# Feed-forward in two parts: hidden activations through DRAM, W_down as seven block products

## The chip, the cores and the metric

One Trainium2 chip, one NeuronCore of it. The number that counts is the device time of one execution of the whole kernel, in microseconds (us). The kernel is a single launch in fp32 data, with every large product done as three bf16 products (high x high, high x low, low x high).

## The reference, cut to what matters

One decoder layer on 2,048 prompt tokens and 64 sample tokens, model width 1,024, hidden width 2,816. The mixer in front (mLSTM heads and dilated attention) is untouched. The change is in the last lines:

```python
hf = rms_norm(x, g_ffn_pre)
f = (jax.nn.silu(hf @ w_gate) * (hf @ w_up)) @ w_down     # 1024 -> 2816 -> 1024
x = x + rms_norm(f, g_ffn_post)
```

## The kernel before

The stages run one after the other; the last, `stage_ffn`, takes about the second half of the span. All of it works on x, transposed in SBUF (`g.x32`, features on partitions in 8 tiles, tokens along the free axis).

**Units.** The hidden width is cut in 22 tiles of 128 columns (m). The prompt's tokens are cut in two pairs of 512-token chunks (q = 0, 1); a unit is one m for one q, so there are 44 units. In a unit the gate and up products of two token chunks, which would be eight block products, are done as seven (`PRODUCTS`, a Strassen-like scheme over [W_gate, W_up] and the token quarters). Each product is 12 matmuls (4 k-tiles x 3 bf16 products) of 128x512. Their order on TensorE is A11, S1, S2, A12, S3, S4, A22. Four of the weight blocks are sums, made by VectorE (`sum_weights`); all seven are split in a high half by ScalarE (`w_split`) and a low half by VectorE. The weight blocks have one buffer each (A22 two), so the next unit's splits are interleaved with this unit's products. Between the products, results leave PSUM: ScalarE copies (`kept`), VectorE adds (`combine_near`, `combine_mid`, `combine_away`), ScalarE does Silu, VectorE multiplies (`hide_away`, `hide_near`). TensorE may start A22 only after `combine_mid`, since both use the same PSUM bank:

```python
pe.wait_ge(combined, 3 * u + 2)
multiply(u, A22, one, False).then_inc(p_done, 1)
```

Units of q = 0 also do the 64 sample tokens: 48 matmuls of 64 columns behind A11.

**Order of the units.** All 22 m with q = 0, then all 22 with q = 1. The seven split weight blocks are therefore made 44 times, and W_gate and W_up are read twice.

**Down.** After each second unit ("part") the two hidden tiles, split in high and low, are multiplied with two row tiles of W_down: 8 token tiles x 2 halves x 2 hidden tiles x 3 = 96 matmuls of 128x512 (`down_tile`), into two PSUM areas of two banks each. VectorE adds each tile's 128x1024 result into SBUF (`add_down`, line 3184). For q = 0 the sample follows (48 narrow matmuls).

**Turnover.** Between q = 0 and q = 1 the token quarters of q = 1 and their sums are made and split (`t_sum_up`, `t_split`, each 128x2048), partly during the last units of q = 0 and between the adds of its last down part (`turn_over`).

**End.** `square` (ScalarE), `inverse_rms` (GpSimd), `finish` (VectorE), `add_to_residual` (a DMA of GpSimd that accumulates in DRAM).

**Queues.** SP loads W_gate and W_up (`load_up`, `load_gate`), each as soon as the splits of the tile before have freed the raw buffer. GpSimd's queue loads W_down. Every engine's instructions are written out in a fixed order and it waits on semaphores in that order.

Of the kernel before, what the change touches and what calls it, by code (L numbers as in the profile page):

```python
# [79 lines left out]
class Sems:  # L80
# [10 lines left out]
    def give_back(self):  # L91

        self._nc.clear_and_free_semaphores(self._taken)
        self._nc.all_engine_barrier()
        self._taken = []
# [2210 lines left out]
PART = 2  # L2306
PARTS = HIDDEN_TILES // PART
UNITS = N_PAIRS * HIDDEN_TILES
# [353 lines left out]
def stage_ffn(nc, g, sems):  # L2662
# [3 lines left out]
    n_rows = [3, 2]  # L2666
    n_down = [PAIR_TILES + 1, PAIR_TILES]
    pair_of = lambda u: u // HIDDEN_TILES
    w_at = lambda u, j: u * PRODUCTS + W_ORDER.index(j) + 1
    made = lambda u, j: u * PRODUCTS + j + 1  # L2670
    first_row = lambda u: u * n_rows[0] if u < HIDDEN_TILES else HIDDEN_TILES * n_rows[0] + (u - HIDDEN_TILES) * n_rows[1]
    silu_at = lambda u, rows: first_row(u) + 1 + ((SAMPLE, NEAR, AWAY), (NEAR, AWAY))[pair_of(u)].index(rows)
    row_at = lambda u, rows: first_row(u) + 1 + ((SAMPLE, AWAY, NEAR), (AWAY, NEAR))[pair_of(u)].index(rows)
    down_at = lambda q, part: (PARTS * n_down[0] + 1 if q else 0) + part * n_down[q]
    SAMPLE_TURNED = PARTS * n_down[0]
    N_FINAL = TILES + 1
    with ExitStack() as ctx:
        sb = lambda n, s, d=F32: ctx.enter_context(nc.sbuf_tensor(n, s, d))
        two = lambda n, s, d=F32: [sb(f"{n}{i}", s, d) for i in range(2)]
        raw_gate, raw_up, raw_down = g.m_w_raw0, g.m_w_raw1, sb("f_raw_down", [P, D_MODEL])  # L2680
        w_sum_area = sb("f_w_sums", [P, 4 * HK * P])
        w_sum = {j: w_sum_area[:, i * HK * P:(i + 1) * HK * P].rearrange("p (k c) -> p k c", k=HK) for i, j in enumerate((S1, S2, S3, S4))}
        w_hi = [[sb(f"f_w_hi{j}", [P, HK, P], BF16)] * 2 if j != A22 else two(f"f_w_hi{j}_", [P, HK, P], BF16)
                for j in range(PRODUCTS)]
        w_lo = [[sb(f"f_w_lo{j}", [P, HK, P], BF16)] * 2 if j != A22 else two(f"f_w_lo{j}_", [P, HK, P], BF16)
                for j in range(PRODUCTS)]
# [4 lines left out]
        t_hi, t_lo = [{**homes, **{j: sb(f"f_t_{n}{j}", [P, HK, CHUNK], BF16)[:, :, :] for j in (B22, T4)},  # L2691
                       X_S2: s_cells[:, i, :, :], X_SD: s_cells[:, 2 + i, :, :]}
                      for i, (n, homes) in enumerate((("hi", g.t_hi), ("lo", g.t_lo)))]
        y_area = sb("f_sums_then_y", [P, 2 * D_MODEL])
        t_sum = y_area[:, :].rearrange("p (k c) -> p k c", k=HK)
        whole = lambda tile: tile[:, :, :].rearrange("p k c -> p (k c)")
        y_homes = [y_area[:, i * D_MODEL:(i + 1) * D_MODEL] for i in range(2)]
        last_homes = [y_homes[1], y_homes[0], whole(raw_up), whole(raw_gate), w_sum_area[:, 0:D_MODEL], w_sum_area[:, D_MODEL:],
                      raw_down[:, :], g.u_area[:, 0:D_MODEL]]
        y_home = lambda f: y_homes[f % 2] if f <= PAIR_TILES else last_homes[f - PAIR_TILES - 1]  # L2700
        near, mid, away = two("f_near", [P, CHUNK]), two("f_mid", [P, CHUNK]), two("f_away", [P, CHUNK])
        squares = mid[0][:, :].bitcast(BF16)
        s_gate = g.k_new[:, 0:NSAMP]
        h_hi, h_lo = [(sb(f"f_h_{n}", [P, PART * PAIR], BF16)[:, :], g.k_new[:, (1 + i) * NSAMP:(2 + i) * NSAMP].bitcast(BF16))
                      for i, n in enumerate(("hi", "lo"))]
        down_hi, down_lo = [area[:, HK * NTOK:HK * NTOK + PART * D_MODEL].rearrange("p (i c) -> p i c", i=PART)
                            for area in (g.mix_m_hi, g.mix_m_lo)]
        y_s = sb("f_y_s", [NSAMP, D_MODEL])
# [739 lines left out]
```

## Time and profile before

| what | value |
|---|---|
| three timed runs | 2625.64, 2623.40, 2623.57 us (median 2623.57) |
| span of the profiled execution | 2616.7 us |
| the profiled execution's own time | not listed apart; the median lies 6.9 us above the span |
| granted TensorE clock, mean | 0.985 |
| busy: TensorE / VectorE / ScalarE / GpSimd | 96% / 67% / 44% / 9% |
| matmul instructions | 16,971 |
| `stage_ffn`: first to last matmul | about 1288 to 2601 us |

Read it so: the span runs from the first to the last instruction. A matmul of 128x512 is shown with 379 ns, but the next one starts 216 ns later, since matmuls are pipelined; the distance from start to start is what one costs in a row. The same holds on a smaller scale for VectorE (0.69 us shown, 0.60 from start to start). "Idle before, releaser" tells what an instruction waited for.

### The profile page before, as it was taken

The numbers are of one execution on the slowest core, as the hardware profiler recorded it, in microseconds if no ns is written. First come the engines' busy times: TensorE is split into PE (matmuls) and PEld (weight loads), VectorE is DVE, ScalarE is ACT, GpSimd is POOL, SyncE is SP. The second block draws the span as 40 slices with busy tenths as digits, with TensorE's granted clock in tenths as the row PEclk, the third lists the DMA queues.
The fourth block names the chain that finished last, engine by engine and source line by source line (L and its number), as shares of the span: only waits on it lengthen the run. The fifth ranks groups of instructions, "written<-read, shape, count | busy, mean of one in ns | idle before, by whom it ended". The sixth has DMA issues, their size and how long they took to land.

```text
span 2616.7 us, 46148 instructions
## 1 busy us (share of the span) xinstructions
PE 2501.4 (96%) x16971; PEld 1433.1 (55%) x17188; DVE 1745.3 (67%) x3772; ACT 1151.2 (44%) x2671; POOL 246.6 (9%) x630
## 2 busy tenths in 40 slices
PE   7999987899999999899899999999999999999997
PEld 4557765476858677555444444444444444444443
DVE  6658886676766767778666665565577666666665
ACT  5558985454545445433433333322243333333233
POOL 1002220011202112211100000000000000000002
PEclk9999998999999999999999999999999999999999
DMA  6431355601111111444221112111111222222213
GB/s 223 135 97 54 104 141 161 189 18 51 34 42 44 35 35 60 145 142 153 73 73 49 51 55 61 53 49 49 49 49 49 57 74 72 66 71 57 57 53 73
DMA packets 203224, 202.92 MB, mean 78 GB/s; under 512 B 11053, under 2 KB 181048, under 8 KB 201584
## 3 DMA queue, kind: packets, MB, share of 16 engines
q1 hardware_dynamic: 193082, 165.26, 21.1%
q0 software_dynamic: 9920, 34.70, 5.1%
q8 instruction: 139, 2.28, 0.4%
q14 instruction: 83, 0.68, 0.1%
HBM read 156.86 MB, written 43.06 MB: 76 GB/s over the span
## 4 chain that ended last, share of the span: by engine, by line
PE 43%; DVE 4%; ACT 2%; issue 1%; POOL 0%; POOLq 0%; DVEq 0%; ACTq 0%
PE f_bank L2798 9%; PE f_bank L2797 9%; PE f_bank L2799 9%; PE f_ps_y L120 5%; PE f_ps_y L118 5%; PE f_ps_y L119 5%; ACT f_h_hi L2934 1%; DVE act L3184 1%; DVE f_w_lo L3056 1%; DVE f_h_lo L3110 1%; DVE f_away L3132 1%; DVE f_near L3144 1%; ACT f_w_hi L2916 1%; DVE f_away L3137 0%; DVE f_w_sums L3071 0%
## 5 line engine op out<-in xcount | busy, mean ns | idle before, releaser
L3184 DVE TENSOR_TENSOR act<-act,f_ps_y 128x1024 f32<-128x1024 f32 x170 | 201.9, 1189 | 156.2 <-PE f_ps_y L120 156.1
L2798 PE MATMUL f_bank<-mix_m_lo_then_tokens,f_w_hi 128*128 128x512 bf16 x699 | 264.9, 379 | 1.7
L120 PE MATMUL f_ps_y<-mix_m_hi_then_tokens,f_h_lo 128*128 128x512 bf16 x697 | 264.2, 379 | 0.9
L2799 PE MATMUL f_bank<-mix_m_hi_then_tokens,f_w_lo 128*128 128x512 bf16 x697 | 264.2, 379 | 0.3
L118 PE MATMUL f_ps_y<-mix_m_hi_then_tokens,f_h_hi 128*128 128x512 bf16 x686 | 260.2, 379 | 2.7 <-DVE act L3184 0.3
L119 PE MATMUL f_ps_y<-mix_m_lo_then_tokens,f_h_hi 128*128 128x512 bf16 x687 | 260.4, 379 | 0.9
L2797 PE MATMUL f_bank<-mix_m_hi_then_tokens,f_w_hi 128*128 128x512 bf16 x672 | 254.7, 379 | 0.4
L2951 ACT ACTIVATE f_near<-f_bank 128x512 f32<-128x512 f32 x44 | 26.1, 593 | 430.9 <-PE f_ps_y L120 237.8
L3056 DVE TENSOR_TENSOR f_w_lo<-f_w_sums,f_w_hi 128x512 bf16<-128x512 f32 x176 | 120.9, 689 | 124.3 <-ACT f_w_hi L2916 123.7
L118 PE MATMUL m_ps_then_y<-w_in_then_w_out_lo,act 128*128 128x256 bf16 x640 | 174.4, 273 | 0.1
L119 PE MATMUL m_ps_then_y<-w_in_then_w_out_lo,act 128*128 128x256 bf16 x640 | 174.4, 273 | 0.0
L120 PE MATMUL m_ps_then_y<-w_in_then_w_out_lo,act 128*128 128x256 bf16 x640 | 174.4, 273 | 0.0
L2069 DVE SCALAR_TENSOR_TENSOR y_then_w_out<-z_then_patterns,m_hd,y_then_w_out 128x512 f32<-128x512 f32 x120 | 90.2, 752 | 86.1 <-ACT y_then_w_out L1803 83.3
L119 PE MATMUL m_ps_then_y<-act,w_in_then_w_out_lo 128*128 128x512 bf16 (+1 forms) x400 | 131.9, 348 | 6.5 <-DVE w_in_then_w_out_lo L2036 4.9
L2797 PE MATMUL f_bank<-f_t_hi,f_w_hi 128*128 128x512 bf16 x351 | 133.1, 379 | 4.8 <-DVE f_mid L3126 3.4
L2798 PE MATMUL f_bank<-f_t_lo,f_w_hi 128*128 128x512 bf16 x347 | 131.5, 379 | 0.1
L3020 POOL DMA_DIRECT2D f_raw_down<-in_w_down x44 | 24.6, 560 | 1133.5 <-DVE mix_m_lo_then_tokens L3105 1133.1
L3056 DVE TENSOR_TENSOR f_w_lo<-m_w_raw,f_w_hi 128x512 bf16<-128x512 f32 x132 | 87.2, 688 | 64.5 <-ACT f_w_hi L2916 64.5
L120 PE MATMUL m_ps_then_y<-act,w_in_then_w_out_lo 128*128 128x512 bf16 (+1 forms) x394 | 129.1, 348 | 0.0
L118 PE MATMUL m_ps_then_y<-act,w_in_then_w_out_lo 128*128 128x512 bf16 (+1 forms) x382 | 124.9, 346 | 1.0 <-ACT z_then_patterns L1800 0.7
L2799 PE MATMUL f_bank<-f_t_hi,f_w_lo 128*128 128x512 bf16 x325 | 123.2, 379 | 0.3
L118 PEld LDWEIGHTS f_ps_y<-mix_m_hi_then_tokens,f_h_hi 128*128 128x128 bf16 x704 | 68.8, 98 | 93.7 <-DVE act L3184 12.0
(523 smaller groups left out, 6156.6 us busy)
## 6 DMA issues: line engine op xcount, KB each, us to landing
m_w_raw<-in_w_gate SPq DMA_DIRECT2D x44, 512.0 KB, 4.2
m_w_raw<-in_w_up SPq DMA_DIRECT2D x44, 512.0 KB, 3.9
f_raw_down<-in_w_down POOLq DMA_DIRECT2D x44, 512.0 KB, 3.8
m_w_raw<-in_w_in SPq DMA_DIRECT2D x20, 512.0 KB, 6.1
o_x<-in_x_prompt SPq DMA_DIRECT2D x16, 512.0 KB, 4.4
out_y_prompt<-states_then_x SPq DMA_DIRECT2D x16, 512.0 KB, 3.0
pattern_rows<-a_stage SPq DMA_DIRECT2D x48, 132.0 KB, 2.1
u_then_w_out_then_tokens<-u_rows SPq DMA_DIRECT2D x5, 1024.0 KB, 4.4
```

The costliest lines, as they stand in the source:

```text
L118: pe.matmul(out, w_hi, x_hi, start=first, stop=False, skip_group_check=in_parts)
L119: pe.matmul(out, w_hi, x_lo, start=False, stop=False, skip_group_check=in_parts)
L120: return pe.matmul(out, w_lo, x_hi, start=False, stop=last, skip_group_check=in_parts)
L2069: ins = nc.vector.scalar_tensor_tensor(out, src, w, out, ALU.mult, ALU.add)
L2797: nc.tensor.matmul(bank[:, :], high, t_hi[j][:, k, :], start=first and k == 0, stop=False, skip_group_check=True)
L2798: nc.tensor.matmul(bank[:, :], high, t_lo[j][:, k, :], start=False, stop=False, skip_group_check=True)
L2799: mm = nc.tensor.matmul(bank[:, :], low, t_hi[j][:, k, :], start=False, stop=k == HK - 1, skip_group_check=True)
L2916: nc.scalar.activation(w_hi[j][u % 2][:, :, :], w_from[j], ACT.Copy).then_inc(w_high, 1)
L2934: nc.scalar.activation(h_all(h_hi, u % PART, rows), hidden, ACT.Copy).then_inc(h_high, 1)
L3056: nc.vector.tensor_tensor(w_lo[j][u % 2][:, :, :], w_from[j], w_hi[j][u % 2][:, :, :], ALU.subtract).then_inc(w_low, 1)
L3110: nc.vector.tensor_tensor(low, hidden, high, ALU.subtract).then_inc(h_done, 1)
L3184: nc.vector.tensor_tensor(tile, tile, fresh, ALU.add).then_inc(total_done, 1)
```

## The change

All of it is in `stage_ffn`, with one barrier in front of it.

1. **Order of the units.** m = 0..7 with q = 0 alone; then for m = 8..21 pairs of tiles (m,0), (m,1), (m+1,0), (m+1,1); then m = 0..7 with q = 1 alone. Units that share m in the middle share one weight set (`SET_OF`), so there are 30 sets, not 44. "Solo" units have a set to themselves.
2. **The token quarters of q = 1** are summed and split in units 1 to 6 (`T_STEPS`), into homes of their own.
3. **Hidden activations** are no longer multiplied with W_down at once. Per unit, VectorE sums and ScalarE and VectorE split blocks of them (`hidden_blocks`, `hidden_high`): for even m two blocks (one sum), for odd m five blocks (three sums). SP stores them in DRAM (`store_hidden`).
4. **W_down's four block sums** are made by GpSimd during units 8 to 28 (`sum_down`) and stored in DRAM.
5. **Down as seven products.** After all units: for each of 7 blocks, 8 pairs of token tiles, 11 x 3 matmuls of 128x512 accumulated in one PSUM bank; 6 banks in turn. VectorE adds each 128x512 result into the output tiles (`add_pair`). SP loads the hidden blocks in quarters (`load_hidden`, two DMAs of 720,896 bytes each) into three slots, and 128x512 pieces of W_down or its sums (`load_down`) into four raw buffers; ScalarE and VectorE split the pieces for the next product meanwhile. The first product's 11 pieces are split in the last four units (`TAIL`).
6. The units have two copies of banks 2 and 3, since the down product no longer needs PSUM at the same time.
7. **A barrier** (`give_back`) in front of `stage_ffn` clears and frees the semaphores of the stages before.

The core of the diff:

```diff
-    def give_back(self):
-
-        self._nc.clear_and_free_semaphores(self._taken)
+    def give_back(self, *kept):
+
+        self._nc.clear_and_free_semaphores([s for s in self._taken if not any(s is k for k in kept)])
         self._nc.all_engine_barrier()
...
+SOLO = 8
+UNIT = ([(m, 0) for m in range(SOLO)] + [(m + d, q) for m in range(SOLO, HIDDEN_TILES, 2) for d in range(2) for q in range(N_PAIRS)]
+        + [(m, 1) for m in range(SOLO)])
...
+T_STEPS = {1: [(0, B11), (1, T1)], 2: [(0, T1), (1, T3)], 3: [(0, T3), (0, B21)], 4: [(1, T2), (0, T2)], 5: [(1, T4), (0, T4)], 6: [(0, B22)]}
...
+                def load_hidden(x):
...
+                    sp.wait_ge(h_store[b], 16 * stores_of(b, UNITS if q else LAST_Q0 + 1))
+                    for part, to in enumerate((slot_hi[s], slot_lo[s])):
+                        sp.dma_start(to, g.h_dram[b, q, :, half * 2 + part, :]).then_inc(h_in[s], 16)
...
+                for n in range(UNITS):
+                    if n:
+                        store_hidden(n - 1)
+                    k = SET_OF[n]
+                    if n == USERS[k][-1] and n and k + 2 < N_SETS:
+                        load_up(k + 2)
+                        load_gate(k + 2)
...
+                    if n == UNITS - TAIL:
+                        load_hidden(0)
+                        load_hidden(1)
+                    if n >= UNITS - TAIL:
+                        for i in range((n - UNITS + TAIL) * TAIL_PIECES, min((n - UNITS + TAIL + 1) * TAIL_PIECES, D_PAIRS)):
+                            load_down(i)
...
+                def down_pair(jn, p):
+                    e, x = at_y(jn, p), jn * 4 + p // 2
+                    bank, s = y_bank[e % BANKS], x % H_SLOTS
+                    bank_free(e)
+                    if p % 2 == 0:
+                        pe.wait_ge(h_in[s], 32 * (x // H_SLOTS + 1))
+                    for i in range(D_PAIRS):
+                        if p == 0:
+                            pe.wait_ge(d_low, jn * D_PAIRS + i + 1)
+                        toks = slice(i * 2 * P + p % 2 * P, i * 2 * P + (p % 2 + 1) * P)
+                        mm = product(nc.tensor, bank[:, :], slot_hi[s][:, toks], slot_lo[s][:, toks], d_hi[jn % 2][:, i, :],
+                                     d_lo[jn % 2][:, i, :], i == 0, i == D_PAIRS - 1)
+                    mm.then_inc(y_ready, 1)
...
+                def unit(n):            # ScalarE
...
+                    if n:
+                        hidden_high(n - 1, 0)
+                    act.wait_ge(p_done, made(n, A11))
...
+                    nc.scalar.activation(near[n % SLOTS], bank1[v][:, :], ACT.Copy).then_inc(kept, 1)
...
+                    act.wait_ge(combined, 3 * n + 3)
+                    nc.scalar.activation(away[n % SLOTS], away[n % SLOTS], ACT.Silu).then_inc(silu_done, 1)
+                    if fresh:
+                        w_split(k + 1, S4)
+                    if n >= UNITS - TAIL:
+                        for i in range((n - UNITS + TAIL) * TAIL_PIECES, min((n - UNITS + TAIL + 1) * TAIL_PIECES, D_PAIRS)):
+                            down_high(i)
...
+                def sum_down(i):        # GpSimd; four sums, each stored at once
...
+                    nc.gpsimd.tensor_tensor(down_sum[:, :], b12, b11, ALU.subtract).then_inc(down_step, 1)
+                    pool.wait_ge(down_step, 4 * i + 1)
+                    pool.dma_start(g.down_sums[DOWN_SUMS.index("T1"), i, :, :], down_sum[:, :]).then_inc(down_store, 16)
...
+                def unit(n):            # VectorE
+                    q, k = UNIT[n][1], SET_OF[n]
+                    fresh = n == USERS[k][-1] and k + 1 < N_SETS
+                    hidden_blocks(n - 1)
+                    if n == USERS[k][0] and k + 1 < N_SETS:
+                        w_sum_up(k + 1)
+                    if fresh:
+                        w_split(k + 1, A11)
+                        w_split(k + 1, A22)
+                        w_split(k + 1, S1)
+                        w_split(k + 1, S2)
+                    if q == 0:
+                        sample_hidden(n)
+                    for step in T_STEPS.get(n, ()):
+                        if step[0]:
+                            t_sum_up(step[1])
+                        else:
+                            t_split(1, step[1])
+                    combine_near(n)
+                    if q == 0:
+                        sample_low(n)
+                    if fresh:
+                        w_split(k + 1, A12)
+                    combine_mid(n)
+                    if fresh:
+                        w_split(k + 1, S3)
+                    combine_away(n)
+                    if fresh:
+                        w_split(k + 1, S4)
+                    hide_away(n)
+                    hide_near(n)
+                    if n >= UNITS - TAIL:
...
+                            down_low(i)
...
+            sems.give_back(g.f_gate_in, g.f_up_in, g.t_high, g.t_low, g.t_sums)
```

## Rows read from the trace of the kernel before

**Rows 1.** Windows, q = 1: busy PE, PEld, DVE, ACT, POOL; clock; DMA share; GB/s.
```profile
2043.00:2560.00 517.00, 513.60 (x2339) 232.48 (x2385) 326.71 (x425) 169.29 (x286) 23.82 (x42) 1.00 0.24 64
```
**Rows 2.** Waits in the feed-forward, TensorE and weight loads: us in total, times, longest.
```profile
PE f_bank L2797 <- DVE f_mid L3126: 3.4, 2, 2.6
...
PEld f_ps_y L118 <- DVE act L3184: 12.0, 20, 0.8
```
**Rows 3.** Timeline, TensorE: first matmul of A11 and of S1, unit 24.
```profile
2086.13 0.38 PE L2797 MATMUL f_bank<-u_then_w_out_then_tokens,f_w_hi 128*128 128x512 bf16 x1
...
2088.72 0.38 PE L2797 MATMUL f_bank<-mix_m_hi_then_tokens,f_w_hi 128*128 128x512 bf16 x1
```
**Rows 4.** Chain that ended last (start, us): down parts' first adds, turnover, last add.
```profile
1641.39 1.14 DVE act L3184
...
1702.85 1.14 DVE act L3184
...
1932.89 1.81 ACT u_then_w_out_then_tokens L2923
1934.72 2.15 DVE u_then_w_out_then_tokens L3079
...
2126.65 1.14 DVE act L3184
...
2183.91 1.14 DVE act L3184
...
2601.56 1.23 DVE act L3184
```
**Rows 5.** Timeline, VectorE, unit 24.
```profile
2088.67 0.69 DVE L3071 TENSOR_TENSOR f_w_sums<-m_w_raw 128x512 f32<-128x512 f32 x1
2089.39 0.69 DVE L3071 TENSOR_TENSOR f_w_sums<-f_w_sums,m_w_raw 128x512 f32<-128x512 f32 x1
...
2097.34 0.68 DVE L3120 TENSOR_TENSOR f_near<-f_bank,f_near 128x512 f32<-128x512 f32 x1
2099.24 0.69 DVE L3056 TENSOR_TENSOR f_w_lo<-m_w_raw,f_w_hi 128x512 bf16<-128x512 f32 x1 [1.22 <-ACT f_w_hi L2916]
2099.84 0.68 DVE L3126 TENSOR_TENSOR f_mid<-f_bank,f_mid 128x512 f32<-128x512 f32 x1
...
2101.94 0.69 DVE L3132 TENSOR_TENSOR f_away<-f_bank,f_away 128x512 f32<-128x512 f32 x1 [0.81 <-PE f_bank L2799]
2103.85 0.69 DVE L3056 TENSOR_TENSOR f_w_lo<-f_w_sums,f_w_hi 128x512 bf16<-128x512 f32 x1 [1.22 <-ACT f_w_hi L2916]
2104.46 0.68 DVE L3137 TENSOR_TENSOR f_away<-f_mid,f_away 128x512 f32<-128x512 f32 x1
```
**Rows 6.** Timeline, ScalarE, the same unit.
```profile
2088.92 0.60 ACT L2951 ACTIVATE f_near<-f_bank 128x512 f32<-128x512 f32 x1 [19.21 <-PE f_bank L2799]
...
2098.05 0.63 ACT L2979 ACTIVATE f_near<-f_near 128x512 f32<-128x512 f32 x1 [1.89 <-DVE f_near L3120]
2098.59 0.61 ACT L2916 ACTIVATE f_w_hi<-m_w_raw 128x512 bf16<-128x512 f32 x1
```
**Rows 7.** Page, DMA issues: KB each, median us to landing.
```profile
m_w_raw<-in_w_gate SPq DMA_DIRECT2D x44, 512.0 KB, 4.2
...
a_v<-v_by_key SPq DMA_DIRECT2D x2, 1040.0 KB, 5.8
```
**Rows 8.** Windows: the heaviest DMA traffic, and a gap of TensorE with what followed.
```profile
10.00:20.00 10.00, 6.37 (x30) 4.06 (x30) 8.54 (x14) 7.47 (x15) 0.14 (x1) 1.00 1.02 417
392.00:400.00 8.00, 3.94 (x40) 3.60 (x41) 3.21 (x14) 3.79 (x11) 1.12 (x7) 0.79 0.39 93
```
**Rows 9.** Timeline, TensorE: the first matmul behind that gap.
```profile
396.06 0.19 PE L118 MATMUL a_ps_o<-rows_then_v_then_values,a_pt_hi 128*128 128x65 bf16 x1 [4.23 <-ACT a_stage L719]
```
**Rows 10.** Source view of the one barrier of this kind: the clearing of semaphores.
```profile
L93 POOLq EVENT_SEMAPHORE_RANGE_CLEAR  x1: 634/634/634, 498.2 to 498.2; - x1
```
**Rows 11.** Groups by line, GpSimd: its work on tiles 512 wide.
```profile
L439 POOL COPY a_xn_then_q_cls<-a_x_then_q_st 128x512 bf16<-128x512 bf16 x16 | 18.0, 1123 | 6.1 <-DVE gain_then_q_pairs L866 6.1
```

More of the change, by code:

```diff
@@ L2696, in stage_ffn @@
[L2696 to L2701, printed above, removed]
@@ new lines, in stage_ffn @@
+        near = [hid_area[:, i * PAIR:i * PAIR + CHUNK] for i in range(SLOTS)]
+        away = [hid_area[:, i * PAIR + CHUNK:(i + 1) * PAIR] for i in range(SLOTS)]
+        mid = two("f_mid", [P, CHUNK])
+        squares = mid[0][:, :].bitcast(BF16)
+        h_diff = sb("f_h_diff_then_y_s", [P, CHUNK])
+        y_turned = h_diff[:, :].rearrange("p (k n) -> p k n", k=KT)
+        fifth = [area[:, HK * NTOK:] for area in (g.mix_m_hi, g.mix_m_lo)]
+        h_block = [sb(f"f_h_block{b}", [P, 4, P * 2], BF16)[:, :, :] for b in range(3)]
@@ L2789, in _, with multiply @@
             def _(pe):
[L2790 to L2793 removed]
+                def multiply(n, j, bank, first):
+                    q, k = UNIT[n][1], SET_OF[n]
+                    pe.wait_ge(w_low, w_at(k, j))
+                    if n in (0, FIRST_Q1):
                         pe.wait_ge(t_low, t_at(q, j))
[L2795 to L2800 removed]
@@ L2802, in multiply_sample @@
[L2802 to L2810 removed]
+                    for kt in range(HK):
+                        high, low = w_hi[j][k % 2][:, kt, :], w_lo[j][k % 2][:, kt, :]
+                        nc.tensor.matmul(bank[:, :], high, t_hi[q][j][:, kt, :], start=first and kt == 0, stop=False, skip_group_check=True)
+                        nc.tensor.matmul(bank[:, :], high, t_lo[q][j][:, kt, :], start=False, stop=False, skip_group_check=True)
+                        mm = nc.tensor.matmul(bank[:, :], low, t_hi[q][j][:, kt, :], start=False, stop=kt == HK - 1, skip_group_check=True)
@@ new lines, in multiply, with multiply_sample, sample @@
+                    return mm
+                def multiply_sample(k, j, x, bank, first, last):
+                    for kt in range(HK):
+                        mm = product(nc.tensor, bank, w_hi[j][k % 2][:, kt, :], w_lo[j][k % 2][:, kt, :], t_hi[0][x][:, kt, :],
+                                     t_lo[0][x][:, kt, :], first and kt == 0, last and kt == HK - 1)
+                    return mm
+                def sample(n):
+                    k = SET_OF[n]
+                    pe.wait_ge(w_low, w_at(k, A12))
+                    if n == 0:
```

909 lines of the change are left out of this document (504 added, 405 removed).

## Prediction

> **What bounds the kernel now.** I read the waits first, then windows, then one unit instruction by instruction. In the feed-forward TensorE hardly waits: one window of 517 us has it busy for 513.6 while VectorE is busy for 327 and DMA at a share of 0.24 and 64 GB/s [rows 1]. So the feed-forward lasts as long as its matmuls. A product of 12 matmuls takes 2.59 us from start to start [rows 3], 0.216 us each. A down part follows the next after 61.46 us for q = 0 and 57.26 us for q = 1 [rows 4]; 264 matmuls at 0.216 are 57.02, which leaves 0.24 us lost per part, where the weight loads wait for the adds [rows 2]. The 4.2 us more of q = 0 are 144 narrow sample matmuls, 0.029 each.
>
> **What goes.** The seven units' products stay (44 x 84 matmuls). Down before: 22 parts x 96 = 2112; after: 7 x 8 x 33 = 1848. 264 fewer x 0.216 = **-57.0 us**. The sample keeps its count (1584 narrow ones). The lost 0.24 us at 22 part ends go, since the down product rotates six banks and an add of 0.7 us stands against 33 matmuls of 7.1 us: **-5.3**. The waits of TensorE for `combine_mid` at the turnover go: **-3.4** [rows 2]. The last add is 512 wide, not 1024 (0.69 for 1.23, [rows 4, 5]): **-0.5**. Weight splits of 14 sets go from VectorE and ScalarE; by themselves they are worth nothing, as they lay beside matmuls.
>
> **What the units now cost.** VectorE gets the hidden blocks at the head of each unit. The point that decides is `combine_mid`, which must be over when S4 is: 6 products = 15.55 us behind the unit's start t0, and 16.95 with a sample (48 x 0.029 = 1.4). I lay out VectorE's list by rows: 0.60 per 128x512 instruction, 0.72 where it needs the one before [rows 5], ScalarE 0.52 to 0.54 [rows 6], and from `combine_near`'s start to `combine_mid`'s end 3.18 (Silu, high and low half of A12 lie between: 2097.34 to 2100.52, [rows 5]). `hide_near` of the unit before starts 0.8 behind t0 (`combine_away` 2101.94, its successors to 2104.46, then one slot).
>
> Solo unit, odd tile before it (eight instructions of blocks): `hide_near` 0.8 to 1.5; sums S1, S2, two low halves and S4 to 4.65; low halves of S1, S2 to 5.9; the high half of S4 stands in ScalarE's list behind the copy of product S1 (5.4), so its low half starts at 6.55; four weight sums to 9.7; four splits to 12.1; `combine_mid` over at 15.28. Limit 15.55: it holds, by 0.27. After an even tile (three instructions) it holds by over 1 us. The middle units, with a shared set, have sums and splits in different units and over 2 us spare. Units 1 to 6 also have one or two `t_sum_up` / `t_split` in front of `combine_near`, 2.2 us each (2.15, [rows 4]), their high halves 1.8 to 1.9 on ScalarE behind the split of S2 (10.4). With a sample ScalarE's copies come up to 1.4 later and VectorE waits for them, so it comes to these steps at 11.2 (odd n, three instructions of blocks) or 13.6 (even n, eight):
>
> - n = 1: high half of B11 at 12.3, split 14.5, sum 16.7, `combine_mid` 19.9: 3.0 over the limit 16.95
> - n = 2: 13.6 + 4.4 = 18.0, 21.2: 4.3
> - n = 3: high half at 12.3, two splits 16.7: 3.0
> - n = 4: sum 15.8, high half after it 17.8, split 20.1, 23.2: 6.3
> - n = 5: sum 13.5, high half 15.5, split 17.7, 20.9: 4.0
> - n = 6: 15.8, 19.0: 2.0
>
> Together **+22.6**, less than +15 only if the lists overlap better than in rows, +27 if each handoff is late. The same sum for the last unit of q = 0 before, which has two such instructions, gives 2.5 us; the trace has 2.6 as the longest wait [rows 2]. That is my check of the method.
>
> **The last four units.** At unit 40 SP issues in order: W_gate for set 28 (which waits for the low half of A12, 14.7 behind t0), four hidden loads of 0.72 MB, three pieces of W_down of 0.26 MB. ScalarE's list ends the unit with `down_high(0)`, which waits for the first piece, and behind it stand the hidden blocks and the copy `near` of unit 41, without which S2 cannot start (5.2 behind its t0). 4.2 MB lie before or in that burst. From 1040 KB in 5.8 us and 417 GB/s at best [rows 7, 8] I take 320 GB/s: 13 us, plus 1.5 for the last landing. ScalarE is free about 12 us into unit 41, the copy ends at 13.1, S2 starts 7.9 late. Bounds 5 (417 GB/s) and 12 (250). In unit 42 the 1.8 us of low halves, a little late themselves, meet the margin of 0.27: 2. Together **+10**.
>
> **Clock.** A gap of 4.2 us was followed by a granted clock of 0.79 of 8 us, though idle time and full speed are in that mean [rows 8, 9]. Five gaps of 4 us or more arise (units 2, 4, 5, 41, the barrier); I take 1 us for each, since part of the slow time gives VectorE room: **+4.5**, between 0 and 10.
>
> **Barrier.** 0.63 us for the clearing [rows 10] and drains around it: **+1.5**, between 1 and 4.
>
> **At nothing.** The 512-wide pieces and adds of the down product: 11 splits and 8 adds, some 14 us of VectorE per 57 us product. Stores of hidden blocks: SP is free between two loads. Down's transfers: per product 4 x 1.44 + 11 x 0.26 = 8.6 MB in 57 us, 151 GB/s; the loads run two quarters (14 us each) ahead. If a piece lands late, VectorE's adds queue behind it, covered by six banks. If that cover were gone, each us of lateness would count.
>
> GpSimd's 44 sums are nowhere in the trace; a copy 512 wide took it 1.12 us [rows 11]. They fall in units with spare time on VectorE. Bounds 0 and, were each to hold VectorE for 1.12 us, four per two units against 1.7 us spare: 2.8 x 11 = 31. I take 0, as `combine_near` and `combine_mid` read only one SBUF operand and the sums come in units without splits. The Trainium skill, "SBUF — State Buffer", "Who interferes with whom", speaks against this edit: a VectorE instruction with two SBUF inputs and a GpSimd one that reads SBUF block each other for the whole instruction, and `tensor_tensor` in GpSimd ("GPSIMD Engine Reference") is about half as fast as VectorE's, an estimate of 1.2 us here. By that rule rival B's 10 us would come true; no row of this trace shows such a meeting.
>
> **Sum.** -57.0 - 5.3 - 3.4 - 0.5 + 22.6 + 10 + 4.5 + 1.5 = -27.6. Against the profiled span of 2616.7 that is 2589.1; the median of the timed runs stands 6.9 above the span, so **2596 us**.
>
> **Rivals.**
> A, the stalls do not come: VectorE's order leaves more room, the burst lands in time. -57.0 - 5.3 - 3.4 - 0.5 + 1.5 = -64.7: 2559 us. For it: TensorE never waited long before. Against: the check at the turnover. Chance 0.06.
> B, GpSimd's sums hold VectorE in the middle units: about 10 us (a third of the bound), 2606; with its bound 2627. For it: VectorE has some 16 instructions of 0.60 in each unit of 18.1 us there, more than half its time. Against: the spare time. Chance 0.14.
> C, slower: the down product is bound by its transfers. It takes 415 us of matmuls, sample included, and reads 60 MB. At 130 GB/s it would take 463 us, 48 more: 2644. The gain is gone below 136 GB/s (60 MB in 443 us). For it: two loads and the pieces share one queue, and weight loads of 512 KB land in 4.2 us, 125 GB/s one by one [rows 7]. Against: the 417 GB/s, and several are in flight. Chance 0.08.
> D, the change does not do what it says: the units wait for each other through the DRAM stores (an `h_block` has one buffer), 2 us in each of 44 units: +88, 2684. Against: a store has over 10 us. Chance 0.02.
> My forecast, 2586 to 2608: 0.70.
>
> **Range.** 2584 to 2614: it takes in the bounds of the stalls (-8, +5), the burst (-3, +6), the clock (-4.5, +5.5), and B's likely size. What a measurement of this kernel can tell from no change is about 0.2%, 5 us. Faster by more: forecast, A and most of B, 0.85; within: 0.05; slower: 0.10.
>
> **What would show it.** Matmuls of 128x512 fewer by 264. Waits of TensorE for `f_mid` of 20 to 27 us, in units 1 to 6 alone, unit 4 the longest. One wait of 5 to 12 us in the fourth unit from the end, for ScalarE's copy, ScalarE itself waiting for a DMA into the W_down pieces. Pairs of the down product 7.13 us apart. It would be wrong if even solo units wait at `f_mid` (the margin of 0.27), if the down pairs are further apart, or if GpSimd's sums lengthen VectorE's instructions in units 8 to 28.

## The result, and the profile after

The changed kernel takes **2597.05 us** (median; 2591.45 to 2600.82) beside 2624.61 for the kernel before on the same chip: a ratio of 0.9901, with a 95% interval from 0.9875 to 0.9927, 27.6 us less by the medians. The forecast was 2596 us, also 27.6 less.

The two profiled spans differ by 19.1 us only (2597.6 for 2616.7). The rest lies ahead of the change: over the profiles of this study the last transpose before the feed-forward starts anywhere between 1283.1 and 1291.3 us, here 3.85 us later in the changed kernel than in the one before. So from here on a kernel's **stage** is what I compare: from the start of that transpose to the start of the last add of a product into `g.x32`. Timeline of TensorE, before:
```profile
1284.26 1.11 PE L2428 MATMUL o_turned<-ident,y_then_w_out 64*128 64x64 f32 x8 [7.10 <-DVE y_then_w_out L2650]
1288.13 0.63 PE L2798 MATMUL f_bank<-u_then_w_out_then_tokens,f_w_hi 128*128 128x512 bf16 x1 [2.76 <-DVE f_w_lo L3056]
```
The same of the kernel after, and VectorE's last add, which answers to the last of [rows 4]:
```profile
1288.11 1.11 PE L2473 MATMUL o_turned<-ident,y_then_w_out 64*128 64x64 f32 x8 [7.09 <-DVE y_then_w_out L2695]
1293.41 0.63 PE L2948 MATMUL f_bank<-u_then_w_out_then_tokens,f_sums_and_w_then_down 128*128 128x512 bf16 x1 [4.18 <-DVE f_sums_and_w_then_down L3231]
...
2582.49 0.69 DVE L3443 TENSOR_TENSOR act<-f_bank,act 128x512 f32<-128x512 f32 x1 [5.24 <-PE f_bank L120]
```
Before: 2601.56 - 1284.26 = 1317.30 us; after: 2582.49 - 1288.11 = 1294.38, **22.9 less**. From the transpose to the first product it is 5.30 us where it was 3.87: the barrier, 1.4.

Waits of TensorE in the stage after (us in total, times, longest), which answer to [rows 2]:
```profile
PE f_bank L2947 <- DVE f_mid L3333: 22.6, 7, 6.2
PE f_bank L2948 <- ACT f_hidden_then_hidden L3083: 7.7, 1, 7.7
...
PE f_bank L2948 <- DVE f_sums_and_w_then_down L3231: 4.2, 1, 4.2
PE f_bank_gate L118 <- DVE table L3254: 1.0, 1, 1.0
```
The first two rows add up to 30.3 us of waits. Windows after (busy PE, PEld, DVE, ACT, POOL; granted clock; DMA share; GB/s): units 1 to 5, the middle from unit 6 on, the last units with the turn into the down product, and the down product:
```profile
1310.00:1450.00 140.00, 119.36 (x748) 56.33 (x759) 102.44 (x144) 60.30 (x102) 0.00 (x0) 0.91 0.28 80
1450.00:2040.00 590.00, 584.83 (x3287) 277.92 (x3347) 356.75 (x552) 227.35 (x420) 97.01 (x110) 1.00 0.40 119
...
2100.00:2180.00 80.00, 71.37 (x431) 33.97 (x437) 47.45 (x77) 32.47 (x57) 0.00 (x0) 0.96 0.47 151
2180.00:2560.00 380.00, 378.10 (x2073) 179.06 (x2107) 92.54 (x134) 58.77 (x99) 24.41 (x38) 1.00 0.49 157
```
In the middle TensorE is busy for 584.8 of 590 us, unit 6's wait of 2.0 us included, and in the down product for 378.1 of 380, nearly as in [rows 1]. The rest of the loss sits in the first and third row, and there the clock is below 1.00 as well. The longest wait is unit 4's. VectorE there (timeline, one line per instruction: start, us, idle before), and TensorE behind it:
```profile
1402.65 2.29 DVE L3276 TENSOR_TENSOR act<-act 128x2048 f32<-128x2048 f32 x1
1406.91 2.29 DVE L3254 TENSOR_TENSOR act<-act 128x2048 bf16<-128x2048 f32 x1 [1.98 <-ACT act L3060]
1409.12 0.68 DVE L3327 TENSOR_TENSOR f_hidden_then_hidden<-f_bank,f_hidden_then_hidden 128x512 f32<-128x512 f32 x1
...
1411.63 0.68 DVE L3333 TENSOR_TENSOR f_mid<-f_bank,f_mid 128x512 f32<-128x512 f32 x1
```
```profile
1412.37 0.61 PE L2947 MATMUL f_bank<-f_t_then_hidden,f_sums_and_w_then_down 128*128 128x512 bf16 x1 [6.22 <-DVE f_mid L3333]
1412.77 0.63 PE L2948 MATMUL f_bank<-f_t_then_hidden,f_sums_and_w_then_down 128*128 128x512 bf16 x1
1413.20 0.63 PE L2949 MATMUL f_bank<-f_t_then_hidden,f_sums_and_w_then_down 128*128 128x512 bf16 x1
...
1416.44 0.38 PE L2948 MATMUL f_bank<-f_t_then_hidden,f_sums_and_w_then_down 128*128 128x512 bf16 x1
```
The rows are the sum of T2, the low half after 1.98 us of waiting for ScalarE's high half, `combine_near` and `combine_mid`: just the list of the prediction. Behind the gap the matmuls start 0.427 us apart, at the lower of the clock's two levels (1.2 GHz), before they return to 0.216. Such runs are 13 (unit 2), 8 (3), 9 (4), 13 (5) and 9 matmuls (unit 41) long; the gap of 2.87 us in unit 1 left none. Over 0.216 us for each matmul they took 2.75 + 1.7 + 1.9 + 2.8 + 2.0 = **11 us**, those counted in part in which the level changes.

### The profile page after: what moved, and what is told of

Its sections match the earlier page's. It is cut to its first block and busy times, and to the rows that moved or that the text cites. A ratio compares the mean times of both kernels' runs of the same rounds, so it can differ in the third digit from the quotient of the medians.

```text
span 2597.6 us, 45864 instructions
## 1 busy us (share of the span) xinstructions
PE 2454.0 (94%) x16716; PEld 1411.0 (54%) x16924; DVE 1574.9 (61%) x3679; ACT 1138.5 (44%) x2680; POOL 321.6 (12%) x696
## 3 DMA queue, kind: packets, MB, share of 16 engines
q1 hardware_dynamic: 264426, 251.52, 31.4%
## 5 line engine op out<-in xcount | busy, mean ns | idle before, releaser
L2948 PE MATMUL f_bank<-act,f_sums_and_w_then_down 128*128 128x512 bf16 x382 | 145.6, 381 | 8.5 <-ACT f_hidden_then_hidden L3083 7.7
L2949 PE MATMUL f_bank<-act,f_sums_and_w_then_down 128*128 128x512 bf16 x395 | 150.5, 381 | 0.9
L2947 PE MATMUL f_bank<-act,f_sums_and_w_then_down 128*128 128x512 bf16 x384 | 146.3, 381 | 0.9 <-DVE f_mid L3333 0.6
L2948 PE MATMUL f_bank<-mix_m_lo_then_tokens,f_sums_and_w_then_down 128*128 128x512 bf16 x320 | 121.3, 379 | 0.9
L2949 PE MATMUL f_bank<-mix_m_hi_then_tokens,f_sums_and_w_then_down 128*128 128x512 bf16 x320 | 121.3, 379 | 0.0
L701 ACT ACTIVATE a_probs<-a_probs,a_low 128x256 f32<-128x256 f32 (+1 forms) x288 | 114.7, 463 | 5.3 <-DVE a_low L885 4.5
L3231 DVE TENSOR_TENSOR f_sums_and_w_then_down<-f_sums_and_w_then_down 128x512 bf16<-128x512 f32 x120 | 82.0, 690 | 54.4 <-ACT f_sums_and_w_then_down L3053 52.7
L2947 PE MATMUL f_bank<-mix_m_hi_then_tokens,f_sums_and_w_then_down 128*128 128x512 bf16 x302 | 114.5, 379 | 0.0
L897 DVE TENSOR_TENSOR a_pt_lo<-a_ps_t,a_pt_hi 128x512 bf16<-128x512 f32 (+1 forms) x120 | 78.8, 657 | 43.1 <-ACT a_pt_hi L711 41.5
L885 DVE CUSTOM_DVE_ANT_0 a_probs<-a_ps_s,m_w_raw 128x256 f32<-128x256 f32 (+1 forms) x288 | 91.0, 361 | 1.1 <-PE a_ps_s L559 0.4
L3118 ACT ACTIVATE f_hidden_then_hidden<-f_hidden_then_hidden 128x512 f32<-128x512 f32 x44 | 27.7, 630 | 139.9 <-DVE f_hidden_then_hidden L3339 139.9
L2947 PE MATMUL f_bank<-f_t_then_hidden,f_sums_and_w_then_down 128*128 128x512 bf16 x160 | 64.1, 400 | 22.9 <-DVE f_mid L3333 22.0
L3053 ACT ACTIVATE f_sums_and_w_then_down<-f_sums_and_w_then_down 128x512 bf16<-128x512 f32 x120 | 74.4, 621 | 23.1 <-PE f_bank L2949 13.4
```

The source lines that it names most:

```text
L701: last = nc.scalar.activation(here, here, ACT.Exp, bias=low[:, u % LOWS, j:j + 1], scale=-1.0)
L885: last = nc.vector.tensor_tensor_reduce(probs[u % PROBS][:, at:at + n], ps_s[u % 2][:, at:at + n], bias[k % 2][:, a, off:off + n], -1.0, 3e38,
L897: nc.vector.tensor_tensor(pt_lo[u % PT][:, 0:n], ps_t[u % TURNED][:, 0:n], pt_hi[u % PT][:, 0:n], ALU.subtract).then_inc(p_done, 1)
L2947: nc.tensor.matmul(bank[:, :], high, t_hi[q][j][:, kt, :], start=first and kt == 0, stop=False, skip_group_check=True)
L2948: nc.tensor.matmul(bank[:, :], high, t_lo[q][j][:, kt, :], start=False, stop=False, skip_group_check=True)
L2949: mm = nc.tensor.matmul(bank[:, :], low, t_hi[q][j][:, kt, :], start=False, stop=kt == HK - 1, skip_group_check=True)
```

## The experiments

Each was timed in turns with the kernel before on its chip (median of before 2619.73 to 2623.04 us on the experiments' chips). "Stage" is from one profile of each kernel, in us, so one to two microseconds between two stages mean nothing until the rows show where they lie.

| kernel | median us | ratio to before, 95% | stage |
|---|---|---|---|
| before | 2624.61 | 1 | 1317.30 |
| changed | 2597.05 | 0.9901 (0.9875 to 0.9927) | 1294.38 |
| pieces first | 2586.65 | 0.9863 (0.9844 to 0.9883) | 1285.35 |
| token steps spread | 2563.43 | 0.9784 (0.9768 to 0.9801) | 1262.95 |
| both | 2554.89 | 0.9747 (0.9729 to 0.9765) | 1253.06 |
| no GpSimd sums | 2600.16 | 0.9922 (0.9908 to 0.9937) | 1295.84 |
| filled gaps | 2586.02 | 0.9871 (0.985 to 0.9891) | 1284.33 |
| hidden rows copied too | 2588.9 | 0.9882 (0.9853 to 0.9911) | 1285.15 |
| before, with the barrier | 2622.91 | 1.0008 (0.9994 to 1.0022) | 1319.87 |
| low halves behind | 2576.02 | 0.9832 (0.9808 to 0.9856) | 1274.73 |
| sums in solo units | 2565.93 | 0.9788 (0.9766 to 0.981) | 1264.76 |
| warm start | 2558.95 | 0.9753 (0.973 to 0.9777) | 1253.09 |

**The burst.** In the changed kernel ScalarE waits for the first piece of W_down, and its next copy, for which S2 of unit 41 waits, stands behind it (timeline of ScalarE):
```profile
2111.94 1.96 ACT L3132 ACTIVATE mix_m_hi_then_tokens<-u_then_w_out_then_tokens 128x512 bf16<-128x512 f32 x3 [10.05 <-DMA u_then_w_out_then_tokens<-in_w_down]
...
2114.32 0.57 ACT L3083 ACTIVATE f_hidden_then_hidden<-f_bank 128x512 f32<-128x512 f32 x1
```
In the experiment SP issues the pieces at the head of the last four units:
```
                     k = SET_OF[n]
+                    if n >= UNITS - TAIL:
+                        for i in ...: load_down(i)
                     if n == USERS[k][-1] and n and k + 2 < N_SETS:
                         load_up(k + 2)
                         load_gate(k + 2)
...
                     if n == UNITS - TAIL:
                         load_hidden(0)
                         load_hidden(1)
-                    if n >= UNITS - TAIL:
-                        for i in ...: load_down(i)
```


> The three pieces of W_down that ScalarE waits for at the end of the fourth unit from the end are issued before the gate and up loads and before the four hidden loads. Theory (the burst is a queue in front of the piece): TensorE's wait of 7.7 us for ScalarE's copy falls below 1 us, the 9 slow matmuls behind it go with it (2.0 us), unit 42's 0.6 us too: about 10 us less than the changed kernel, 2587 us. Rival (the piece waits for something else than the transfers issued before it, such as its own DMA time under load): the wait stays above 4 us and the time within 4 us of the changed kernel's 2597.

The stage is 9.0 us shorter. The 7.7 us are gone, and so are the slow matmuls (2.0) behind them: the window 2100 to 2180 now shows the full clock. That would be 9.7; but in this execution unit 1's gap, 2.87 us as before, was followed by slow matmuls (1.3 us), and units 2 to 5 had 0.6 us less of them.
```profile
2100.00:2180.00 80.00, 78.96 (x475) 37.93 (x481) 50.86 (x82) 35.67 (x64) 0.00 (x0) 1.00 0.50 163
```
Its one wait of TensorE between 2000 and 2200:
```profile
PE f_bank L2947 <- DVE f_mid L3333: 0.6, 1, 0.6
```
So the burst was a queue in front of one piece. Whether the hidden loads or the weight loads in that queue mattered more is open, since the pieces went ahead of both. Unit 42's 0.6 us stayed, which I had put down to the burst wrongly.

**The token steps.** Three sums go into the hidden blocks of an even tile, all else behind `combine_mid`, one instruction to a unit:
```
+T_EARLY = {1: T1, 3: T3, 5: T2}
+T_STEPS = {1: [(0, B11)], 2: [(0, T1)], 3: [(0, T3)], 4: [(0, B21)], 5: [(0, T2)], 6: [(1, T4)], 7: [(0, T4)], 8: [(0, B22)]}
...
                         keep_low(n, H_A11)
+                        if n + 1 in T_EARLY:
+                            t_sum_up(T_EARLY[n + 1])
                         keep_low(n, H_S3)
...
-                    for step in T_STEPS.get(n, ()): ...
                     combine_near(n)
...
                     combine_mid(n)
                     if fresh:
                         w_split(k + 1, S3)
+                    for step in T_STEPS.get(n, ()): ...
```


> VectorE's sums and low halves of the tokens of q = 1 leave their place in front of combine_near: three of the four sums go between the low halves of the hidden blocks of an even tile, everything else goes behind combine_mid, one instruction in each unit up to unit 8. Theory (these instructions in front of combine_mid are the whole wait): the six waits for f_mid, 22.6 us together, fall below 4 us, and the slow matmuls behind them (9.1 us after the gaps in units 2 to 5) go as well: 26 to 31 us less than the changed kernel, about 2569 us. Rival (the waits come from ScalarE's late copies and would move to hide_near or to the weight splits): under 12 us less, with new waits of TensorE for the weights or for f_bank1 in units 2 to 9.

The stage is 31.4 us shorter: 21.7 us of waits and 9.1 of slow matmuls are 30.8. Of the waits for `f_mid` 0.9 us are left: unit 42's 0.6, and 0.3 in unit 9, which is new:
```profile
PE f_bank L2948 <- DVE f_mid L3336: 0.9, 2, 0.6
```
Where only the low halves move, in the same units (`t_split(1, j)` behind `combine_mid(n)`, the sums where they were):

> Of the instructions in front of combine_near only the low halves move behind combine_mid, in the same units; the four sums stay. By my layout combine_mid is then late by 2.1 us in units 2 and 4 alone (a sum behind eight instructions of hidden blocks); what is moved makes VectorE start the next unit up to 4.4 us later, of which its wait for ScalarE's copies takes up some 1.5 each. Theory (place and number both count): the waits for f_mid fall from 22.6 us to 6 to 12, 15 to 24 us less than the changed kernel with the slow matmuls behind them. Rival (only the place counts): waits of 4 us or less and 26 us less or more. Rival (only the number of instructions in a unit counts): waits of 18 us or more.

```profile
PE f_bank L2947 <- DVE f_mid L3333: 8.3, 4, 4.6
```
The waits are 8.3 us and the stage is 19.7 us shorter: place and number both count. My layout had 2.1 us in units 2 and 4 alone. Unit 2 had 2.0, but unit 4 had 4.6, and unit 5, where none was forecast, 1.0 (unit 42's 0.6 is in the sum too). In unit 4 the sum of T2 is still in front, and ScalarE's high half of it, which waits for the sum, stands ahead of the high half of the sample, for which VectorE then waits for 1.5 us (timeline of ScalarE):
```profile
1392.68 1.91 ACT L3060 ACTIVATE act<-act 128x2048 bf16<-128x2048 f32 x1 [5.04 <-DVE act L3276]
```

**Both edits.**

> Both edits. If the two stalls are independent, their gains add: 36 to 41 us less than the changed kernel, about 2559 us, 65 less than the kernel before, which is what the fewer matmuls, part ends and turnover waits are worth without any stall (rival A of the prediction). If a common cause such as the clock ties them, the sum falls short by over 4 us.

The stage is 41.3 us shorter than the changed kernel's, 9.0 + 31.4 = 40.4 by parts: the stalls are independent. Against the kernel before it is 64.2 us shorter, and by the prediction's terms without stalls 57.0 + 5.3 + 3.4 + 0.5 - 1.4 (barrier) - 0.9 (the waits left) = 63.9. That supports the sum of these terms; no run separates them. Its ratio is 0.9747 (0.9729 to 0.9765), the best here.

**The clock.** In the changed kernel TensorE fills its own gaps, with VectorE's lists untouched:
```
+FILL = {1: 12, 2: 18, 3: 12, 4: 28, 5: 17, 6: 8}
...
                     multiply(n, S4, bank3[v], False).then_inc(p_done, 1)
+                    for i in range(FILL.get(n, 0)):
+                        nc.tensor.matmul(bank2[1 - v], w_hi[A22][SET_OF[n] % 2][:, i % HK, :], t_hi[UNIT[n][1]][T4][:, i % HK, :], ...)
                     pe.wait_ge(combined, 3 * n + 2)
```


> The changed kernel with TensorE's idle time in units 1 to 6 filled: behind S4, before it waits for combine_mid, it runs 12, 18, 12, 28, 17 and 8 more matmuls of 128x512 into a PSUM bank that nobody reads then (0.216 us each, somewhat shorter than each gap). VectorE's lists stay as they are. Theory (the slow matmuls behind the gaps come of TensorE's idleness and are a cost of its own): A22 starts where it did, the 9 to 13 matmuls at 0.427 us behind the gaps of units 2 to 5 run at 0.216, and the stage is 9 us shorter than the changed kernel's. Rival (that time is not lost, since the lists of VectorE behind it are late anyway): under 3 us less, the waits for f_mid growing in the following units instead.

The stage is 10.1 us shorter although TensorE computes 95 matmuls more. Timeline of TensorE, unit 4:
```profile
1402.71 2.97 PE L2990 MATMUL f_banks_then_turned<-f_t_then_hidden,f_sums_and_w_then_down 128*128 128x512 bf16 x13
1405.86 0.39 PE L2948 MATMUL f_bank<-f_t_then_hidden,f_sums_and_w_then_down 128*128 128x512 bf16 x1 [0.18 <-DVE f_mid L3337]
1406.09 0.38 PE L2949 MATMUL f_bank<-f_t_then_hidden,f_sums_and_w_then_down 128*128 128x512 bf16 x1
```
```profile
1310.00:1450.00 140.00, 137.98 (x875) 66.76 (x888) 108.92 (x156) 66.02 (x112) 0.00 (x0) 1.00 0.31 89
```
A22 starts as late as VectorE lets it, and the matmuls behind the gap are 0.216 us apart. The wait at unit 41 was 6.3 us here for 7.7, so some 8.7 us are the slow matmuls': the cost of the clock is its own, beside that of the waits.

**The start.** Nine matmuls ahead of the first product, in both edits' kernel:
```
+                x = t_hi[0][B11]
+                pe.wait_ge(t_low, t_at(0, B11))
+                for i in range(9):
+                    nc.tensor.matmul(bank1[1][:, :], x[:, i % HK, 0:P], x[:, i % HK, :], ...)
                 for n in range(UNITS):
                     unit(n)
```


> The kernel with both edits, and ahead of its first product nine matmuls of 128x512 on token blocks that are there already, into a bank that unit 1 clears, in the 4.2 us in which TensorE waits for the first low half of the weights (0.427 us each at the low clock level, 3.8 us). If the eleven or twelve slow matmuls of the first product come of that idle time, most of them run at 0.216 us and the stage gets 1 to 2.4 us shorter; but VectorE's splits may bound the first unit, in which case the 2.4 us turn into waits and nothing is gained. I expect 1 us less, 2 at most.

The first product runs at the full clock, and nothing is gained where I had expected 1 us: 1253.09 for 1253.06 us. From the transpose to the sample's first matmul it is 10.54 us with and without, since that one waits for VectorE's splits. Slow matmuls cost only where TensorE is the bound.

**GpSimd's sums.** The four `tensor_tensor` are left out, and unsummed blocks are stored in place of the sums, so this kernel leaves out a part of the computation (the first of the four):
```
-                    nc.gpsimd.tensor_tensor(down_sum[:, :], b12, b11, ALU.subtract).then_inc(down_step, 1)
+                    pool.sem_inc(down_step, 1)
                     pool.wait_ge(down_step, 4 * i + 1)
-                    pool.dma_start(g.down_sums[DOWN_SUMS.index("T1"), i, :, :], down_sum[:, :]).then_inc(down_store, 16)
+                    pool.dma_start(g.down_sums[DOWN_SUMS.index("T1"), i, :, :], b12).then_inc(down_store, 16)
...
```


> GpSimd's 44 subtractions of W_down blocks are left out: its loads and stores stay, and unsummed blocks are stored in place of the sums, so that part of the computation is missing. Theory (the sums cost nothing): within 3 us of the changed kernel, 2597 us, although VectorE's few lengthened instructions in units 8 to 28 return to 0.6 us. Rival B of the prediction (the sums hold VectorE where it counts): about 10 us less, 2587 us.

The stage is 1.5 us longer, not shorter, and the intervals of the ratios overlap. The 1.5 are not the sums': unit 1's gap of 2.87 us was followed in this execution by 8 slow matmuls (1.7 us), in the changed kernel's by none. VectorE was busy for 344.6 us in the window 1450 to 2040 where it was for 356.8, so the sums do lengthen its instructions, by 12.2 us together. Groups by line, `hide_away`, changed kernel and then without the sums (busy us, mean ns, idle before):
```profile
L3344 DVE TENSOR_TENSOR f_hidden_then_hidden<-f_mid,f_hidden_then_hidden 128x512 f32<-128x512 f32 x31 | 26.8, 864 | 9.7 <-ACT f_hidden_then_hidden L3118 9.7
```
```profile
L3344 DVE TENSOR_TENSOR f_hidden_then_hidden<-f_mid,f_hidden_then_hidden 128x512 f32<-128x512 f32 x31 | 21.3, 687 | 9.7 <-ACT f_hidden_then_hidden L3118 9.7
```
The rest of the 12.2 is nearly all `sample_low` (L3321). Which instructions lengthen can be read too. In the changed kernel 28 of VectorE's instructions with an input in PSUM, `combine_near` and `combine_mid` (16) among them, lie beside one of GpSimd's subtractions for over 0.1 us, and each took 0.68 or 0.69 us. The 15 with both inputs in SBUF were longer than alone, every one. Timeline of GpSimd, then of VectorE, `combine_near` and `sample_low` (0.22 alone):
```profile
1797.73 1.26 POOL L3190 TENSOR_TENSOR f_down_sum<-act 128x512 f32<-128x512 f32 x1 [6.11 <-DMA act<-in_w_down]
```
```profile
1797.75 0.69 DVE L3327 TENSOR_TENSOR f_hidden_then_hidden<-f_bank,f_hidden_then_hidden 128x512 f32<-128x512 f32 x1 [0.75 <-PE f_bank L2949]
1798.36 0.72 DVE L3321 TENSOR_TENSOR f_hs<-k_new_then_mix_s,f_hs 128x64 bf16<-128x64 f32 x1
```
Is the lengthening harmless by nature, or by place? To both edits' kernel 32 such instructions are added, where VectorE has little room:
```
+                for n in range(UNITS - SOLO, UNITS):
+                    pool.wait_ge(p_done, made(n, A11))
+                    for i in range(4):
+                        nc.gpsimd.tensor_tensor(down_sum[:, :], down_sum[:, :], down_sum[:, :], ALU.subtract).then_inc(load_step, 1)
```


> The kernel with both edits, and four more GpSimd subtractions of 128x512 (scratch data, 1.26 us each) in each of the last eight units, from the end of product A11 on, where VectorE works at its hidden blocks. There VectorE's margin before combine_mid is 0.27 us behind an odd tile and about 1 us behind an even one. Theory (GpSimd and VectorE do hold each other up, and the sums of the change were free only because units 8 to 28 have over 2 us spare): VectorE's instructions that they meet lengthen by 0.6 to 1 us, up to 3 us in a unit, TensorE waits for f_mid in these units, and the time is 5 to 17 us above the kernel with both edits. Rival (the meetings are too short to matter anywhere): within 2 us of it.

The stage is 11.7 us longer. Timeline of GpSimd and of VectorE in unit 36:
```profile
1982.45 5.86 POOL L3229 TENSOR_TENSOR f_down_sum<-f_down_sum 128x512 f32<-128x512 f32 x4 [133.65 <-PE f_bank L2951]
```
```profile
1982.39 0.68 DVE L3289 TENSOR_TENSOR mix_m_hi_then_tokens<-f_hidden_then_hidden,mix_m_hi_then_tokens 128x512 bf16<-128x512 f32 x1
1982.99 1.53 DVE L3289 TENSOR_TENSOR mix_m_lo_then_tokens<-f_hidden_then_hidden,mix_m_lo_then_tokens 128x512 bf16<-128x512 f32 x1
1984.44 1.52 DVE L3306 TENSOR_TENSOR f_hidden_then_hidden<-f_hidden_then_hidden 128x512 f32<-128x512 f32 x1
...
1987.33 1.52 DVE L3289 TENSOR_TENSOR f_h_block<-f_hidden_then_hidden,f_h_block 128x512 bf16<-128x512 f32 x1
1988.78 0.68 DVE L3289 TENSOR_TENSOR mix_m_lo_then_tokens<-f_hidden_then_hidden,mix_m_lo_then_tokens 128x512 bf16<-128x512 f32 x1
```
Here an instruction with two SBUF inputs that starts beside one of GpSimd's takes 1.45 us from start to start for 0.60, and four in a row make the rest of the list late. Then TensorE waits in two places:
```profile
PE f_bank L2949 <- ACT f_hidden_then_hidden L3104: 6.6, 4, 2.9
PE f_bank L2949 <- DVE f_mid L3344: 4.7, 5, 1.0
```
Together they are 11.3 us. Only the second is the wait that I had expected. The larger goes through ScalarE, in units 36, 38, 40 and 42: VectorE's first weight sum is late, ScalarE's high half of it starts as the sum ends and stands ahead of the copy of product S2, and S3 waits for that copy (VectorE, ScalarE and TensorE in unit 36):
```profile
1989.38 0.68 DVE L3255 TENSOR_TENSOR f_sums_and_w_then_down<-m_w_raw 128x512 f32<-128x512 f32 x1
```
```profile
1990.09 0.63 ACT L3055 ACTIVATE f_sums_and_w_then_down<-f_sums_and_w_then_down 128x512 bf16<-128x512 f32 x1 [3.46 <-PE f_bank L2951]
1990.63 0.58 ACT L3104 ACTIVATE f_hidden_then_hidden<-f_bank 128x512 f32<-128x512 f32 x1
```
```profile
1991.26 0.39 PE L2949 MATMUL f_bank<-act,f_sums_and_w_then_down 128*128 128x512 bf16 x1 [1.21 <-ACT f_hidden_then_hidden L3104]
```
The Trainium skill ("SBUF — State Buffer", "Who interferes with whom") has the two engines exclude each other on a shared pair of ports; these rows agree that the two take turns, with +0.85 us for each meeting here; that the ports are the reason no row can show.

**The transfers.** Behind each load of hidden blocks the same rows are copied once more, DRAM to DRAM, on the kernel with the pieces first:
```
                         sp.dma_start(to, g.h_dram[b, q, :, half * 2 + part, :]).then_inc(h_in[s], 16)
+                        sp.dma_start(g.h_again[x, part, :, :], g.h_dram[b, q, :, half * 2 + part, :]).then_inc(again, 16)
```


> The kernel with the pieces issued first, and behind each load of hidden blocks a copy of the same rows from DRAM to DRAM on the same queue: 28 x 2 x 0.72 MB more, so about 260 GB/s in place of 157 in the down product. If the down product has the room that the 417 GB/s of the kernel before suggest, TensorE waits under 2 us in it and the time is within 4 us of the kernel with the pieces first (2587 us). Rival C of the prediction (the product is near the bound of its transfers): waits of TensorE for the hidden slots or the W_down halves of more than 20 us.

```profile
2170.00:2550.00 380.00, 378.11 (x2073) 179.07 (x2108) 92.36 (x134) 58.35 (x99) 25.11 (x38) 1.00 0.74 256
```
At 256 GB/s TensorE is as busy as at 157, and the stage is 0.2 us shorter than without the copies: the down product has some 100 GB/s to spare.

**The barrier.** The kernel before with `sems.give_back(g.f_gate_in, g.f_up_in, g.t_high, g.t_low, g.t_sums)` between `stage_mix_out` and `stage_ffn`:

> The kernel before with one part of the change alone: the clearing of semaphores and the barrier of all engines ahead of the feed-forward. By the changed kernel's trace 1.4 us from the last o_turned transpose to the first product, perhaps with a few slow matmuls more: 1 to 4 us slower than before. Rival (the barrier is hidden by the first weight splits, and the 1.4 us came of the new order): the same time within 0.5 us between these two instructions.

```profile
1291.25 1.11 PE L2428 MATMUL o_turned<-ident,y_then_w_out 64*128 64x64 f32 x8 [7.10 <-DVE y_then_w_out L2650]
1296.54 0.63 PE L2798 MATMUL f_bank<-u_then_w_out_then_tokens,f_w_hi 128*128 128x512 bf16 x1 [4.18 <-DVE f_w_lo L3056]
```
From the transpose to the first product it is 5.29 us, as in the changed kernel: the barrier's 1.4. The sample's first matmul starts 1.4 later too (10.54 for 9.12 behind the transpose), so the slow matmuls between cost nothing. The stage is 2.6 us longer. The other 1.2 are not the barrier's either: the gap of 2.57 us at the turnover was followed here by 7 slow matmuls, in the kernel before by none. First matmul behind that gap, with the barrier and then before (0.61 us for 0.39):
```profile
1952.98 0.61 PE L2797 MATMUL f_bank<-f_t_hi,f_w_hi 128*128 128x512 bf16 x1 [2.57 <-DVE f_mid L3126]
```
```profile
1944.56 0.39 PE L2797 MATMUL f_bank<-f_t_hi,f_w_hi 128*128 128x512 bf16 x1 [2.57 <-DVE f_mid L3126]
```
The medians alone (+0.08%, -0.06 to +0.22) can't tell the barrier from nothing.

## Why the prediction was right

**What goes.** Matmuls, part ends, turnover waits and last add, 66.2 us by the prediction, carried the result: both edits' kernel, without stalls, shows 64.2 of them net of barrier and rest where 63.9 follow. The weight loads, one for each matmul, fell by just 264 (17,188 to 16,924 on the two pages). Pairs of the down product start at 2182.01, 2189.13 and 2196.26: 7.13 and 7.12 us apart, forecast 7.13.

**Units 1 to 6.** Forecast 3.0, 4.3, 3.0, 6.3, 4.0 and 2.0, together 22.6; measured 2.87, 4.16, 2.87, 6.22, 3.87 and 2.0, together 22.0. Counting VectorE's list by durations from another unit, with each handoff to ScalarE, gave every gap to 0.15 us. No solo unit waited at `f_mid` but unit 42 (0.6), so the margin of 0.27 held but for that one.

**The last four units.** 7.9 forecast at unit 41, 7.7 measured. For unit 42 the forecast was 2, and 0.6 came, which the pieces issued first did not change. TensorE's wait is in the third unit from the end, as the prediction's layout has it, and not in the fourth, as its last paragraph says; ScalarE's begins at the end of the fourth.

**The clock: the step that was mis-sized.** "I take 1 us for each" was 2.75, 1.9, 2.8 and 2.0 for the gaps that were forecast at 4 us and more, in units 2, 4, 5 and 41, and the 2.9 us gap of unit 3, which I had not counted, cost 1.7. Instead of 4.5 us (five at 1 us would be 5) it is 11, beyond the upper bound of 10. I read a mean clock of 0.79 over a window with idle time in it [rows 8]; the start-to-start distances behind the gap, 0.427 for 0.216, are the view that gives the price. Nor did it give VectorE room: filling the gaps returned 8.7 of the 9.1 us in units 2 to 5. The fifth gap, the barrier, has its slow matmuls where VectorE bounds, and they cost nothing.

**The barrier.** 1.5 forecast, 1.4 measured.

**At nothing.** The new pieces and adds of VectorE, the stores of hidden blocks and the loads cost TensorE nothing: 378.1 of 380 us busy in the down product, 584.8 of 590 in the middle. A subtraction of GpSimd took 1.26 to 1.29 us.

**The stage's sum.** -66.2 + 22.0 + 0.6 + 7.7 + 11 + 1.4 = -23.5; measured -22.9. The prediction had -27.6: 6.5 us too little for the clock, 2.4 too much elsewhere, and 0.6 that the terms leave open. That the medians fell by just 27.6 us is partly luck, as the interval of the ratio is 19.2 to 32.8 us. By the stage the kernel gained 4.7 us less than forecast. "The median of the timed runs stands 6.9 above the span" hides such a spread: in each later run the time is 1.8 or 1.9 us above its own span, so the profiled execution of before was a quick one, by some 5 us.

**The rivals.** A (2559 us, the stalls do not come) was ruled out by the waits, and came true once they were edited away: 2554.89, which is 64.8 below the kernel before on that chip, forecast 64.7. B's mechanism is real, but its price in units 8 to 28 is nil: VectorE's 12.2 us more fall into its spare time there. Both of my reasons hold: `combine_near` and `combine_mid` kept their 0.69 us beside GpSimd's subtractions, and where there is no spare time, in the solo units, 32 such subtractions cost 11.7 us. C is refuted with 100 GB/s to spare, D by the middle window.

## What to carry to other kernels

Work that an engine off the bound takes on is priced by its ordered list up to the one instruction that the bound engine waits for, unit by unit, and a long instruction is placed behind that point, not spread by count alone. A gap in a bound TensorE costs its length and then up to 2.8 us of half-speed matmuls, so the five gaps of 2.9 to 6.2 us in units 1 to 5, 20.0 us together, cost nearly half as much again. Before a transfer that ends a unit's list is put behind others on a queue, ask who waits for it: three small loads moved ahead of four large ones and the weight loads gave 9 us.

## What the runs showed that I had not expected

A gap of 2.87 us left no slow matmul in unit 1, and one of the same length left eight in unit 3. Nor does the place decide: unit 1's gap, 2.87 us each time, left none in the changed kernel's profile, 7 slow matmuls with the pieces first and 8 without GpSimd's sums. The turnover's gap of 2.57 us left none before and 7 with the barrier, and one of 2.04 us (low halves behind, unit 2) left 8. So a short gap's price differs between executions by 1.3 to 1.7 us, and what decides it these runs don't show. First matmul behind unit 1's gap, changed kernel and then pieces first:
```profile
1335.56 0.39 PE L2947 MATMUL f_bank<-f_t_then_hidden,f_sums_and_w_then_down 128*128 128x512 bf16 x1 [2.87 <-DVE f_mid L3333]
```
```profile
1338.55 0.61 PE L2947 MATMUL f_bank<-f_t_then_hidden,f_sums_and_w_then_down 128*128 128x512 bf16 x1 [2.87 <-DVE f_mid L3333]
```
And VectorE and GpSimd took turns to the end of each instruction: four subtractions of GpSimd took 5.86 us beside four of VectorE, 1.46 each, where one alone takes 1.26.
